# Half a block of split-precision weights beside each attention unit: the sparse queries' projection and half of the output projection moved

## The chip, the core and the metric

One core of a Trainium2 chip runs the whole program. The metric is the time of one execution in microseconds (us) on the device. Engines: TensorE (PE, its weight loads PEld), VectorE (DVE), ScalarE (ACT), GpSimd (POOL) and SyncE (SP), which issues nearly all transfers.

## The reference, cut to what matters

A decoder trunk of two layers over 272 tokens (16 meta tokens and 256) of width 2048, in float32:

```python
proj = h @ w_in        # u | fq fk fv | ff | dq | ckv | iq ik iw
y_ssm = _s5_mixer(u, ...)                    # state space, then a gate g @ glu_w
y_fox = _fox_attention(fq, fk, fv, ff)       # 8 heads of 64, forgetting bias
dk, dv = jnp.split(_rms_norm(ckv) @ w_kv_up, 2)
dq, dk, iq, ik = (_partial_rope(t) for t in (dq, dk, iq, ik))
y_dsa = _dsa_attention(dq, dk, dv, iq, ik, iw, topk=64)   # keys chosen by an indexer
y = concat(rms(y_ssm), rms(y_fox), rms(y_dsa))            # 1024 | 512 | 512
h = layer_norm(ALPHA * h + y @ w_out)
h = layer_norm(ALPHA * h + conv_ffn(h))      # up, causal conv, silu gate, down
```

The softmax of the forgetting attention subtracts a row's maximum, so a term that is the same for every key of a row drops out of it.

## The kernel before, in words

Activations lie with features on the partitions and the 272 tokens along the free axis. All weights come as one stream of blocks of 512 KB (`stream`, in the order of use): a block holds 4 tiles of 128 input features (KB) for 256 output features. Four slots (`raw`) take the blocks in turn. The table `PHASES` gives each phase's output groups and blocks for each group: `in` 17 x 4, `glu` 4 x 2, `out` 8 x 4, `up` 44 x 4, `down` 8 x 11.

For the phases in `SPLIT` the product is made in three parts: ACT rounds the block to `w_hi` (`cast`, L699), DVE makes the remainder (`low_part`, L992), and PE does for each of 4 tiles and 2 halves lo x hi, hi x lo and hi x hi (`split_block`, L383 to L385): 24 matmuls of 128 x 272 for a block. They add up in two PSUM banks. `glu` uses the raw block in plain float32 (L587).

The order of work on each engine is written out by hand, and semaphores tie the engines together. A layer runs:

1. **Input projection with the state space beside it.** 18 steps; the loop deals 4 blocks of `in` to each of the first 16 steps, and puts between them the state space products of chunk m (L424, L434, L456, L465, L470), the rope matmuls (`ROPE_STEPS`, L496, DVE L1290 to L1293) and the products with `w_kv` (L510). Ropes 9 to 12 are those of the sparse queries dq, 13 to 16 those of the sparse keys, in steps 16 and 17, after the last block.
2. **Indexer and gate.** 48 index scores (L575) and four gate groups (L587).
3. **Attention in 48 units**, 24 of the forgetting kind and then 24 of the sparse kind: 8 heads, each with three query tiles of 96, 96 and 80 rows against 96, 192 and 272 keys. PE does for unit n the scores (L522 to L527, or L530 and L531), the transposes of unit n-2's probabilities (L543) and unit n-3's weighted values (L554). DVE takes the maximum (L1455), scales it (L1457), copies the transposed probabilities from PSUM (L1466), and inverts the denominator (L1469). ACT does the exponential (L888) and stores the output (L897). Beside this DVE picks the top 64 keys for each query in eight rounds (`top_scores`, L1404 and L1407), one in every third unit of the first 24, makes `dsa_bias` from them (`sparse_bias`), and normalises the gated output `yssm` (L1487), ACT and DVE splitting it in two parts (`high_part`, `low_y`). Weights stand still in this stage.
4. **Output projection** (`products` with phase `out`): 8 groups of 4 blocks, the first two blocks of each on the gated half of y, the third on the forgetting, the fourth on the sparse outputs. DVE's `residual` (L1083, L1087, L1100) adds ALPHA times the old h, which is kept as x_hi and x_lo, and sums h over the first 12 tiles in `hsum`. PE sums that over the partitions (L369) after group 6; DVE subtracts this pivot (`take_pivot`, L1015) and folds squares (L1025 to L1029), before the residual of group 7.
5. The layer norm, the MLP (`up`, `down`), and the second layer norm.

The first forgetting score product of a unit is followed by `pe.matmul(s, cum[:, qs:ke], sel_r...)` (L524), which adds the query's own cumulative gate to each key, and by L525, which subtracts the key's.

## Time and profile before

| | us |
|---|---|
| median of 3 runs | 2813.67 (2808.85 to 2813.9) |
| the profiled execution's own time | 2811.41 |
| its span, first to last instruction | 2809.6 |
| PE busy | 2668.1 (95%) |
| PEld busy | 2548.4 (91%) |
| DVE busy | 1782.2 (63%) |
| ACT busy | 1366.1 (49%) |
| mean granted TensorE clock | 0.938 |

The durations of matmuls overlap, since they are pipelined: what one costs in a dense stretch is the distance from its start to the next one's. The granted clock is a share of 2.4 GHz: 1.00 is 2.4, 0.50 is 1.2 GHz. The two layers pass the same stages, the second some 1400 us after the first.

### The profile page before, as it was taken

What the parts mean: (1) busy time and instruction counts of PE and PEld (TensorE: products, weight loads), DVE (VectorE), ACT (ScalarE), POOL (GpSimd) and SP (SyncE); (2) the same over time, 40 slices, a digit from 0 to 9 for tenths busy, and PEclk for the clock granted to TensorE, in tenths of its full rate; (3) what the DMA queues carried; (4) which work ended last, traced back from release to release, by engine and by line L of the source; (5) the groups of instructions that cost most, each with busy time, mean ns of one, the idle gap of its engine ahead of it and who ended that gap; (6) DMA issues with size and microseconds to landing.
All of it is one profiled execution on the core that took longest, in us unless ns stands there. A gap on an engine that the chain in (4) does not pass through costs nothing.

```text
span 2809.6 us, 56056 instructions
## 1 busy us (share of the span) xinstructions
PE 2668.1 (95%) x21786; PEld 2548.4 (91%) x21786; DVE 1782.2 (63%) x2890; ACT 1366.1 (49%) x2051; POOL 11.9 (0%) x19
## 2 busy tenths in 40 slices
PE   5989999989999999999979899999899999999997
PEld 5989866989999999999979898669899999999997
DVE  6777555576666666544487775655766666665445
ACT  5444443456555555433364444444566665653333
POOL 0000000000000000000000000000000000000000
PEclk8999975899999999999999999659999999999999
DMA  4433210435555555554444332104355555555553
GB/s 170 146 113 127 76 45 1 150 120 179 179 173 177 172 173 171 180 173 166 165 146 150 107 127 77 38 1 163 115 194 182 182 180 179 184 184 186 173 183 112
DMA packets 109728, 401.84 MB, mean 143 GB/s; under 512 B 12176, under 2 KB 12176, under 8 KB 109584
## 3 DMA queue, kind: packets, MB, share of 16 engines
q1 hardware_dynamic: 108432, 395.15, 41.9%
q0 software_dynamic: 1152, 4.63, 0.4%
q8 instruction: 108, 1.77, 0.3%
q14 instruction: 36, 0.29, 0.0%
HBM read 397.50 MB, written 2.23 MB: 142 GB/s over the span
## 4 chain that ended last, share of the span: by engine, by line
PE 89%; DVE 6%; ACT 3%; issue 2%; DMA 1%; SPq 0%; ACTq 0%; DVEq 0%
PE ps L383 25%; PE ps L384 25%; PE ps L385 25%; PE ps L587 2%; PE ps L554 2%; PE ps L530 1%; PE ps L456 1%; PE ps L522 1%; PE ps L575 1%; PE ps L543 1%; PE ps L465 1%; DVE h L1047 1%; DVE h L1067 1%; ACT h L715 1%; PE ps L531 1%
## 5 line engine op out<-in xcount | busy, mean ns | idle before, releaser
L699 ACT ACTIVATE w_hi<-raw 128x1024 fp32r<-128x1024 f32 x728 | 763.6, 1057 | 935.3 <-PE ps L385 918.0
L384 PE MATMUL ps<-x_lo,w_hi 128*128 128x272 f32 (+1 forms) x3904 | 1122.1, 287 | 0.0
L385 PE MATMUL ps<-x_hi,w_hi 128*128 128x272 f32 (+1 forms) x3904 | 1120.2, 287 | 0.0
L992 DVE TENSOR_TENSOR w_lo<-raw,w_hi 128x1024 fp32r<-128x1024 f32 x592 | 716.8, 1224 | 616.3 <-ACT w_hi L699 616.2
L383 PE MATMUL ps<-x_hi,w_lo 128*128 128x272 f32 (+1 forms) x2816 | 805.5, 286 | 19.9 <-DVE x_lo L1075 19.3
L384 PEld LDWEIGHTS ps<-x_lo,w_hi 128*128 128x128 f32 x3904 | 741.3, 190 | 1.8
L385 PEld LDWEIGHTS ps<-x_hi,w_hi 128*128 128x128 f32 x3904 | 741.1, 190 | 0.0
L383 PEld LDWEIGHTS ps<-x_hi,w_lo 128*128 128x128 f32 x2816 | 530.8, 189 | 21.8 <-issue 19.2
L383 PE MATMUL ps<-g_hi,w_lo 128*128 128x272 f32 (+1 forms) x1408 | 403.9, 287 | 4.8 <-DVE w_lo L992 2.7
L384 PE MATMUL ps<-g_lo,w_hi 128*128 128x272 f32 (+1 forms) x1408 | 403.2, 286 | 0.0
L385 PE MATMUL ps<-g_hi,w_hi 128*128 128x272 f32 (+1 forms) x1408 | 401.2, 285 | 0.0
L383 PEld LDWEIGHTS ps<-g_hi,w_lo 128*128 128x128 f32 x1408 | 266.9, 190 | 5.3 <-DVE w_lo L992 2.9
L385 PEld LDWEIGHTS ps<-g_hi,w_hi 128*128 128x128 f32 x1408 | 268.3, 191 | 0.0
L384 PEld LDWEIGHTS ps<-g_lo,w_hi 128*128 128x128 f32 x1408 | 266.8, 189 | 0.2
L383 PE MATMUL ps<-x_hi,in_lo_a 128*128 128x272 f32 x544 | 169.2, 311 | 23.6 <-DVE x_lo L1075 15.3
L383 PE MATMUL ps<-x_hi,in_lo_b 128*128 128x272 f32 x544 | 163.6, 301 | 0.0
L1532 DVE SCALAR_TENSOR_TENSOR conv<-ps,cpar,conv 128x271 f32<-128x271 f32 (+1 forms) x352 | 159.4, 494 | 3.1
L383 PE MATMUL ps<-y_hi,w_lo 128*128 128x272 f32 x512 | 150.4, 294 | 0.7 <-DVE w_lo L992 0.7
L385 PE MATMUL ps<-y_hi,w_hi 128*128 128x272 f32 x512 | 149.5, 292 | 0.0
L383 PEld LDWEIGHTS ps<-x_hi,in_lo_a 128*128 128x128 f32 x544 | 107.8, 198 | 27.4 <-issue 25.0
L992 DVE TENSOR_TENSOR in_lo_b<-raw,w_hi 128x1024 fp32r<-128x1024 f32 x68 | 83.2, 1224 | 67.9 <-ACT w_hi L699 67.7
L383 PEld LDWEIGHTS ps<-x_hi,in_lo_b 128*128 128x128 f32 x544 | 102.2, 188 | 5.4 <-issue 3.2
(257 smaller groups left out, 2977.6 us busy)
## 6 DMA issues: line engine op xcount, KB each, us to landing
raw<-stream SPq DMA_DIRECT2D x744, 512.0 KB, 3.3
h<-x SPq DMA_DIRECT2D x4, 544.0 KB, 6.2
out<-h SPq DMA_DIRECT2D x4, 544.0 KB, 2.7
cst<-consts POOLq DMA_DIRECT2D x2, 724.0 KB, 6.4
wkv<-w_kv POOLq DMA_DIRECT2D x2, 512.0 KB, 7.8
b_st<-ssm_b POOLq DMA_DIRECT2D x2, 512.0 KB, 9.2
c_st<-ssm_c POOLq DMA_DIRECT2D x2, 512.0 KB, 11.4
par<-params SPq DMA_DIRECT2D x1, 562.0 KB, 12.0
```

Source lines behind the costliest of these rows:

```text
L383: pe.matmul(acc, lo_w[:, kk, cols], hi, start=k == 0, stop=False)
L384: pe.matmul(acc, w_hi[:, slot, kk, cols], lo, start=False, stop=False)
L385: mm = pe.matmul(acc, w_hi[:, slot, kk, cols], hi, start=False, stop=k == tiles - 1)
L456: mm = pe.matmul(ps[:, 4 + e, c * NJ:c * NJ + NJ], abt[rows, s, c, :], proj[rows, U0 + m, s * NJ:s * NJ + NJ], start=s == 0, stop=s == CH - 1)
L465: pe.matmul(ps[:, 6, k * NJ:NT], kexp[:, k, :, :].rearrange("p e q -> p (e q)"), proj[:, U0 + m, 0:(CH - k) * NJ], start=k == 0, stop=False)
L522: pe.matmul(s, proj[b, FQ0 + hd // 2, qs:ke], proj[b, FK0 + hd // 2, 0:ke], start=True, stop=False)
L530: pe.matmul(s, proj[b, DQ0 + hd // 2, qs:ke], kv[b, hd // 2, 0:ke], start=True, stop=False)
L554: mm = pe.matmul(ps[0:qn, 7, 0:HEAD], pt[0:kn, n % 2, q - c, 0:qn], v_tok[0:kn, kind, c, hd * HEAD:hd * HEAD + HEAD], start=c == 0, stop=c ...
L587: mm = pe.matmul(ps[:, 2 * (g % 2) + j, 0:NT], raw[:, n % SLOTS, kk, j * P:j * P + P], proj[:, U0 + k, :], start=k == 0, stop=k == 7)
L699: act.activation(w_hi[:, slot, :, :], raw[:, slot, :, :], ACT.Copy).then_inc(hi_made, 1)
L992: dve.tensor_tensor(w_low(phase, slot), raw[:, slot, :, :], w_hi[:, slot, :, :].bitcast(F32), ALU.subtract).then_inc(in_lo_made if phase = ...
L1532: last = dve.scalar_tensor_tensor(out=cv[:, j, tap:NT], in0=ps[:, 2 * odd + j, 0:NT - tap], scalar=cpar[:, odd, 2 + 2 * tap + j:3 + 2 * ta ...
```

## The change

Eight of the 68 blocks of the input projection, those of the sparse queries dq, become a phase `late` (2 groups of 4 blocks); the output projection is cut into a phase `gated` (8 groups of 2 blocks, the gated half of y) and `out` (8 groups of 2, the attended half). Both new phases run inside attention: beside each unit PE does half a block, `late` in units 0 to 15, `gated` in units 16 to 47. ACT casts and DVE makes low parts one or two units ahead, into three areas `gated_w` and not `w_lo`, and one pair of PSUM banks, 0 and 1, takes all these groups. ACT moves a finished `late` group to `proj` in units 7 and 15, and the four dq ropes follow in units 9, 10, 17 and 18. DVE ends each `gated` group with the ALPHA terms of the residual, so that `out` adds only its own sum. The input projection then runs in 17 steps that take 7 blocks in two. In the first 24 units the copy of the transposed probabilities goes from DVE to ACT, the maximum is negated in the same instruction (the scale 1/8 goes into the queries when PSUM is read, and the factor 8 in `sel` is dropped), and L524's product is removed. Line numbers of the changed kernel are higher: 407 to 409 answer to 383 to 385, 1063 to 992.

```diff
-PHASES = {"in": (17, DT // KB, 1), "glu": (4, UT // KB, 4), "out": (8, DT // KB, 4),
-          "up": (FT, DT // KB, 2), "down": (8, FT // KB, 4)}
-SPLIT = ("in", "out", "up", "down")
+PHASES = {"in": (15, DT // KB, 1), "glu": (4, UT // KB, 4), "late": (2, DT // KB, 2), "gated": (8, UT // KB, 4),
+          "out": (8, UT // KB, 4), "up": (FT, DT // KB, 2), "down": (8, FT // KB, 4)}
...
+
+
+def blocks_at(step, pos):
+
+    n = 4 + 7 * (step // 2) + 4 * (step % 2) + pos
+    return [n] if n < BLOCKS_IN and not (step % 2 and pos == 3) else []
+
...
+
+ROPE_STEPS = {6: (0,), 7: (1, 2), 8: (3, 4), 9: (5, 6), 10: (7, 8), 15: (9, 10), 16: (11, 12)}
 ROPES = 17
-MS_STEP = 5
-KV_STEPS = {12: (0, 1), 13: (2, 3), 14: (4, 5), 15: (6, 7)}
+LATE_ROPES = {9: 13, 10: 14, 17: 15, 18: 16}
+MS_STEP = 6
+KV_STEPS = {11: (0, 1), 12: (2, 3), 13: (4, 5), 14: (6, 7)}
...
+GATED_FROM = 16
 FOX_NORM = UNITS // 2 + 3
...
+            def late_half(l, n):
+
+                g, b = n // 8, n // 2 % 4
+                if n % 8 == 0:
+                    pe.wait_ge(psum_free, first_group(l, "late") + g + 2)
+                pe.wait_ge(lo_made, first_low(l, "late") + n // 2 + 1)
+                split_block("late", (first_block(l, "late") + n // 2) % SLOTS, b, 0, DT, x_parts, part=range(2 * (n % 2), 2 * (n % 2) + 2))
+
+            def gated_half(l, n):
+
+                g, b = n // 4, n // 2 % 2
+                if n % 4 == 0:
+                    pe.wait_ge(psum_free, first_group(l, "gated") + g + 2)
+                pe.wait_ge(lo_made, first_low(l, "gated") + n // 2 + 1)
+                split_block("gated", (first_block(l, "gated") + n // 2) % SLOTS, b, 0, UT, lambda k: (y_hi[:, k, :], y_lo[0][:, k, :]),
+                            (lambda k: (ylo_made, 4 * l + k // 4 + 1)) if n < 4 else None, part=range(2 * (n % 2), 2 * (n % 2) + 2))
+
+            def late_rope(l, r):
+
+                pe.wait_ge(roped, l * ROPES + r)
+                if r == 13:
+                    pe.wait_ge(glu_sd, l + 1)
+                pe.wait_ge(psum_free, first_group(l, "late") + (r - 13) // 2 + 1 + 2)
+                pe.matmul(ps[:, rope_bank(r), 0:NT], const("perm"), rope_tile(r), start=True, stop=True).then_inc(rot_made, 1)
...
-                    pe.matmul(s, cum[:, qs:ke], sel_r[:, hd:hd + 1].to_broadcast([P, ke]), start=False, stop=False)
...
+                    if n < GATED_FROM:
+                        late_half(l, n)
+                    elif n < UNITS:
+                        gated_half(l, n - GATED_FROM)
+                    if n in LATE_ROPES:
+                        late_rope(l, LATE_ROPES[n])
                     if 2 <= n < UNITS + 2:
...
+                    act.activation(dst, src, ACT.Copy, scale=SCALE if FQ0 <= 2 * g < FQ0 + 4 else 1.0).then_inc(psum_free, 1)
...
+                def half_cast(n):
+
+                    if n % 2 == 0:
+                        if n < GATED_FROM:
+                            cast(l, "late", n // 2)
+                        else:
+                            cast(l, "gated", (n - GATED_FROM) // 2)
...
+                    if 2 <= n < UNITS // 2 + 2:
+                        m = n - 2
+                        q = m % NQ
+                        qn = QT[q][1]
+                        act.wait_ge(ptr_made, l * UNITS + m + 1)
+                        if m >= 2:
+                            act.wait_ge(o_made, l * UNITS + m - 1)
+                        act.activation(pt[0:MASK_T, m % 2, 0:q + 1, 0:qn],
+                                       ps[0:MASK_T, 6, 0:NQ * MASK_T].rearrange("p (c t) -> p c t", c=NQ)[:, 0:q + 1, 0:qn],
+                                       ACT.Copy).then_inc(pt_made, 1)
...
+                        high_part((n - GATE_NORM - 6) // 2)
+                    if n in (7, 15):
+                        g = n // 8
+                        act.wait_ge(block_used, first_block(l, "late") + 4 * (g + 1))
+                        act.activation(proj[:, DQ0 + 2 * g:DQ0 + 2 * g + 2, :], ps[:, 0:2, 0:NT], ACT.Copy, scale=SCALE).then_inc(psum_free, 1)
+                    if n < UNITS - 4:
+                        half_cast(n + 4)
...
                 blocks = PHASES[phase][1]
+                bank = 0 if phase == "gated" else 2 * (g % 2)
                 dve.wait_ge(block_used, first_block(l, phase) + blocks * (g + 1))
-                h2 = h[:, 2 * g:2 * g + 2, :]
-                dve.scalar_tensor_tensor(out=h2, in0=x_lo[:, 2 * g:2 * g + 2, :].bitcast(F32), scalar=ALPHA,
-                                         in1=ps[:, 2 * (g % 2):2 * (g % 2) + 2, 0:NT],
-                                         op0=ALU.mult, op1=ALU.add).then_inc(psum_free, 1)
-                dve.wait_ge(psum_free, first_group(l, phase) + g + 3)
-                mark(dve.scalar_tensor_tensor(out=h2, in0=x_hi[:, 2 * g:2 * g + 2, :].bitcast(F32), scalar=ALPHA, in1=h2,
-                                              op0=ALU.mult, op1=ALU.add))
-                if g < PIVOT // 2:
+                h2, acc = h[:, 2 * g:2 * g + 2, :], ps[:, bank:bank + 2, 0:NT]
+                if phase == "out":
+                    dve.tensor_tensor(h2, h2, acc, ALU.add).then_inc(psum_free, 1)
+                    dve.wait_ge(psum_free, first_group(l, phase) + g + 3)
+                else:
+                    dve.scalar_tensor_tensor(out=h2, in0=x_lo[:, 2 * g:2 * g + 2, :].bitcast(F32), scalar=ALPHA,
+                                             in1=acc, op0=ALU.mult, op1=ALU.add).then_inc(psum_free, 1)
+                    dve.wait_ge(psum_free, first_group(l, phase) + g + 3)
+                    mark(dve.scalar_tensor_tensor(out=h2, in0=x_hi[:, 2 * g:2 * g + 2, :].bitcast(F32), scalar=ALPHA, in1=h2,
+                                                  op0=ALU.mult, op1=ALU.add))
+                if g < PIVOT // 2 and phase != "gated":
...
-                        after()
-                        dve.tensor_scalar(stat[0:qn, 0, n % 4:n % 4 + 1], stat[0:qn, 0, 4 + n % 4:5 + n % 4], -SCALE, None,
-                                          ALU.mult).then_inc(max_made, 1)
+                        dve.reduce_max(stat[0:qn, 0, n % 4:n % 4 + 1], ps[0:qn, S_BANKS[n % 3], 0:qs + qn], AX_X,
+                                       negate=True).then_inc(max_made, 1)
                     if n >= 2:
                         m = n - 2
...
-                        if m >= 2:
+                        if m >= UNITS // 2:
+                            dve.wait_ge(ptr_made, l * UNITS + m + 1)
                             dve.wait_ge(o_made, l * UNITS + m - 1)
-                        dve.tensor_copy(pt[0:MASK_T, m % 2, 0:q + 1, 0:qn],
-                                        ps[0:MASK_T, 6, 0:NQ * MASK_T].rearrange("p (c t) -> p c t", c=NQ)[:, 0:q + 1, 0:qn]
-                                        ).then_inc(pt_made, 1)
+                            dve.tensor_copy(pt[0:MASK_T, m % 2, 0:q + 1, 0:qn],
+                                            ps[0:MASK_T, 6, 0:NQ * MASK_T].rearrange("p (c t) -> p c t", c=NQ)[:, 0:q + 1, 0:qn]
+                                            ).then_inc(pt_made, 1)
+                        else:
+                            dve.wait_ge(prob_made, l * UNITS + m + 1)
...
-                    if GATE_NORM + 4 <= n < GATE_NORM + 12:
-                        k = n - GATE_NORM - 4
-                        last = dve.scalar_tensor_tensor(out=yssm[:, k, :], in0=yssm[:, k, :], scalar=param("mix_g", l * DT + k),
-                                                        in1=rstd[:, :], op0=ALU.mult, op1=ALU.mult)
+                    if GATE_NORM + 4 <= n < GATE_NORM + 8:
+                        for k in range(2 * (n - GATE_NORM - 4), 2 * (n - GATE_NORM - 4) + 2):
...
+                    if n < UNITS - 2:
+                        half_low(n + 2)
+                    if n in LATE_ROPES:
+                        dve.wait_ge(roped, l * ROPES + LATE_ROPES[n])
+                        rope(LATE_ROPES[n])
+                    if n >= GATED_FROM and n % 4 == 3 and n < UNITS:
+                        residual(l, "gated", (n - GATED_FROM) // 4)
...
-                for g in range(8):
-                    for n in range(4):
-                        if g:
-                            low_part(l, "out", 4 * g + n)
-                    if g:
+                for g in range(1, 9):
+                    for n in range(2):
+                        if g < 7:
+                            low_part(l, "out", 2 * g + 2 + n)
+                    if g < 8:
                         residual(l, "out", g - 1)
```

**PE, one unit of the forgetting kind** (the widest query tile): before, its scores, a transpose of unit n-2, and the values of unit n-3.

```order
L522 MATMUL ps<-proj 80x272
L524 MATMUL ps<-sel_r,cum 80x272
L525 MATMUL ps<-cum,sel_r 80x272
L527 MATMUL ps<-causal_r,ident_r 80x80
L543 MATMUL ps<-cst,probs 96x96
L554 MATMUL ps<-v_tok,pt 80x64 x3
```

Now, unit 9, a narrow one, of the changed kernel (L571, L573, L575 are its scores, L560 is a late rope, L591 and L602 transposes and values; the three dense rows come four times):

```order
L571 MATMUL ps<-proj 96x96
L573 MATMUL ps<-cum,sel_r 96x96
L575 MATMUL ps<-causal_r,ident_r 96x96
L407 MATMUL ps<-x_hi,gated_w_73 128x272
L408 MATMUL ps<-x_lo,w_hi 128x272
L409 MATMUL ps<-x_hi,w_hi 128x272
...
L560 MATMUL ps<-proj,cst 128x272
L591 MATMUL ps<-cst,probs 96x96 x2
L602 MATMUL ps<-v_tok,pt 96x64
```

Twelve dense matmuls stand between the scores and the transposes, and one small matmul is gone.

**DVE, unit 8**, before:

```order
L1455 TENSOR_REDUCE stat<-ps 80x1
L1457 TENSOR_SCALAR stat<-stat 80x1
L1466 COPY pt<-ps 96x96
L1469 RECIPROCAL stat<-stat 96x1
L1404 MAX top_88<-work 96x8 x2
L1404 MAX top_88<-work 80x8
L1407 MATCH_REPLACE work<-top_88,work 96x96
L1407 MATCH_REPLACE work<-top_88,work 96x192
L1407 MATCH_REPLACE work<-top_88,work 80x272
L1487 SCALAR_TENSOR_TENSOR yssm<-yssm,par,rstd 128x272
```

and now:

```order
L1538 TENSOR_REDUCE stat<-ps 80x1
L1552 RECIPROCAL stat<-stat 96x1
L1477 MAX top_92<-work 96x8 x2
L1477 MAX top_92<-work 80x8
L1480 MATCH_REPLACE work<-top_92,work 96x96
L1480 MATCH_REPLACE work<-top_92,work 96x192
L1480 MATCH_REPLACE work<-top_92,work 80x272
L1570 SCALAR_TENSOR_TENSOR yssm<-yssm,par,rstd 128x272 x2
L1063 TENSOR_TENSOR gated_w_74<-raw,w_hi 128x1024
```

The scaling and the copy have left; a second normalising product and a low part have come, all ahead of unit 9's maximum.

**DVE, the end of the output projection**, before:

```order
L1100 TENSOR_TENSOR hsum<-hsum,h 128x544
L992 TENSOR_TENSOR w_lo<-raw,w_hi 128x1024 x4
L1083 SCALAR_TENSOR_TENSOR h<-x_lo,ps 128x544
L1087 SCALAR_TENSOR_TENSOR h<-x_hi,h 128x544
L1015 SCALAR_TENSOR_TENSOR h<-ps,h 128x1088 x3
L1015 SCALAR_TENSOR_TENSOR h<-ps,h 128x544
L1025 TENSOR_TENSOR sq_out<-sq_out 128x1088 x2
```

and now:

```order
L1063 TENSOR_TENSOR w_lo<-raw,w_hi 128x1024 x2
L1156 TENSOR_TENSOR h<-h,ps 128x544
L1175 TENSOR_TENSOR hsum<-hsum,h 128x544
L1156 TENSOR_TENSOR h<-h,ps 128x544
L1086 SCALAR_TENSOR_TENSOR h<-ps,h 128x1088 x3
L1086 SCALAR_TENSOR_TENSOR h<-ps,h 128x544
L1096 TENSOR_TENSOR sq_out<-sq_out 128x1088 x2
```

The pivot and the squares are unchanged, and the residual ahead of them has one operation where it had two.

## Rows read from the trace of the kernel before

**Rows 1.** Windows by stage; columns: length, busy by engine, PEclk, DMA share, GB/s

```profile
core 0: us, PE busy (x) PEld busy (x) DVE busy (x) ACT busy (x) POOL busy (x), PEclk, DMA share, GB/s
60.00:323.30 263.30, 251.33 (x2768) 241.74 (x2768) 198.13 (x293) 113.79 (x180) 0.00 (x0) 0.99 0.37 126
323.30:380.90 57.60, 53.40 (x334) 40.76 (x332) 23.02 (x67) 26.35 (x70) 0.00 (x0) 1.00 0.19 65
380.90:498.80 117.90, 111.77 (x496) 80.65 (x496) 70.09 (x308) 49.73 (x167) 0.00 (x0) 0.51 0.02 5
504.70:600.00 95.30, 95.30 (x738) 94.98 (x739) 58.74 (x68) 34.28 (x33) 0.00 (x0) 0.97 0.52 177
```

**Rows 2.** Timeline of PE: three forgetting units late in the stage; start, length

```profile
425.26 0.95 PE L522 MATMUL ps<-proj 64*96 64x192 f32 x2
...
427.82 1.19 PE L522 MATMUL ps<-proj 64*80 64x272 f32 x2
...
429.55 0.38 PE L543 MATMUL ps<-cst,probs 96*96 96x96 f32 x1
...
432.44 0.95 PE L522 MATMUL ps<-proj 64*96 64x192 f32 x2
```

**Rows 3.** Timeline of PE: the first three units, before the clock falls

```profile
380.87 0.38 PE L522 MATMUL ps<-proj 64*96 64x96 f32 x2 [1.05 <-ACT yssm L838]
...
382.45 0.68 PE L522 MATMUL ps<-proj 64*80 64x272 f32 x2
383.06 0.34 PE L524 MATMUL ps<-sel_r,cum 128*80 128x272 f32 x1
383.24 0.29 PE L525 MATMUL ps<-cum,sel_r 128*80 128x272 f32 x1
383.38 0.20 PE L527 MATMUL ps<-causal_r,ident_r 80*80 80x80 f32 x1
```

**Rows 4.** Timeline of PE: from one sparse unit to the third after it

```profile
475.60 0.63 PE L530 MATMUL ps<-kv,proj 64*96 64x96 f32 x2
...
481.90 0.63 PE L530 MATMUL ps<-kv,proj 64*96 64x96 f32 x2
```

**Rows 5.** Timeline of PE: dense matmuls in the input projection, 21 starts apart

```profile
100.74 0.29 PE L385 MATMUL ps<-x_hi,w_hi 128*128 128x272 f32 x1
...
103.35 0.28 PE L385 MATMUL ps<-x_hi,w_hi 128*128 128x272 f32 x1
```

**Rows 6.** Timeline of PE: dense matmuls as the output projection begins, three starts apart

```profile
505.52 0.43 PE L383 MATMUL ps<-y_hi,w_lo 128*128 128x272 f32 x1
...
506.20 0.43 PE L383 MATMUL ps<-y_hi,w_lo 128*128 128x272 f32 x1
```

**Rows 7.** The page's groups, and DVE's timeline: casts, low parts, a round of the top keys

```profile
L699 ACT ACTIVATE w_hi<-raw 128x1024 fp32r<-128x1024 f32 x728 | 763.6, 1057 | 935.3 <-PE ps L385 918.0
L992 DVE TENSOR_TENSOR w_lo<-raw,w_hi 128x1024 fp32r<-128x1024 f32 x592 | 716.8, 1224 | 616.3 <-ACT w_hi L699 616.2
...
430.58 0.84 DVE L1404 MAX8 top<-work 96x8 f32<-96x96 f32 x3
...
432.30 1.28 DVE L1447 TENSOR_TENSOR gated_lo<-yssm,y_hi 128x1088 fp32r<-128x1088 f32 x1
```

**Rows 8.** Timeline of PE and of DVE: the end of the output projection

```profile
591.88 1.08 PE L369 MATMUL ps<-hsum,ones_p 128*128 128x272 f32 x4
...
595.95 4.32 DVE L1015 SCALAR_TENSOR_TENSOR h<-ps,h 128x1088 f32<-128x1088 f32 x4
...
603.73 0.72 DVE L1029 TENSOR_TENSOR sq_out<-sq_out 128x544 f32<-128x544 f32 x1
604.98 0.72 DVE L1083 SCALAR_TENSOR_TENSOR h<-x_lo,ps 128x544 f32<-128x544 f32 x1 [0.53 <-PE ps L385]
```

**Rows 9.** A window of 3 us inside the input projection

```profile
168.00:171.00 3.00, 1.91 (x15) 1.62 (x14) 2.93 (x5) 2.48 (x3) 0.00 (x0) 1.00 0.57 175
```

**Rows 10.** Timeline of PE: the wait for the sparse bias

```profile
441.42 0.64 PE L530 MATMUL ps<-kv,proj 64*96 64x96 f32 x2 [3.01 <-DVE dsa_bias L1420]
```

188 lines of the change are left out of this document (97 added, 91 removed).

## Prediction

> **What bounds the kernel now.** I read the stages first, then the starts on TensorE inside them. The windows by stage [rows 1] show PE busy for 251 of 263 us in the input projection, and for all of 95 us in the output projection, at a granted clock near 1.00: there the path is PE's stream of dense matmuls, and DVE (198 of 263) and ACT (114) have room. In attention PE is busy for 112 of 118 us too, but the clock is 0.51, and DVE (70) and ACT (50) are half idle, and almost nothing is loaded. So attention is bound by small matmuls at 1.2 GHz. Three units of the forgetting kind take 432.44 - 425.26 = 7.18 us [rows 2], three sparse ones 6.30 [rows 4].
>
> The clock was 1.00 through the indexer stage [rows 1]. The first units still ran at it: the widest tile's four score products take from 382.45 to 383.58, 1.13 us [rows 3]; the same products late in the stage take from 427.82 to 429.55, 1.73 us [rows 2]. So a unit at full clock takes 1.13 / 1.73 = 0.65 of its time at half clock.
>
> A dense matmul costs (103.35 - 100.74) / 21 = 0.124 us at full clock [rows 5], a block of 24 of them 2.98. At half clock it costs (506.20 - 505.52) / 3 = 0.227 [rows 6].
>
> **The change part by part**, for one layer, then doubled (the second layer runs the same code; only its MLP differs).
>
> *Input projection.* 8 blocks leave: 8 x 2.98 = -23.9. Four rope matmul pairs leave, about as long as the widest plain float32 score product (382.45 to 383.06, 0.6 [rows 3]): -2.4. PE was busy 95% of the stage, so most of this is on the path, but the state space work on DVE stays, with one low part less (1.22 [rows 7]) in each pair of steps, and PE has to wait for its results sooner. 3 us inside the stage show how that looks: PE busy 1.91, DVE 2.93 [rows 9]. I give back 2. Together -25; the bounds are -18 (each pair of steps keeps a further us) and -28 (all of it, and a shorter tail with two dk ropes behind the last block in place of four).
>
> *Output projection.* 16 blocks leave: 16 x 2.98 = -47.8. Two things come late now. After group 6, PE sums the pivot (591.88, 1.08), and DVE then subtracts it and folds squares from 595.95 to 604.45 (603.73 + 0.72), 8.5 us, before the residual of group 7; that residual waited only 0.53 more for PE, which had 12 us of group 7 to do [rows 8]. Group 7 is now 6 us. PE is ready at 591.9 + 1.1 + 6.0 = 599.0, DVE at 593.1 + 8.5 = 601.6: 2.6 us come back, less 0.7 for a residual that has one operation. At the beginning only one block, not three, covers the split of the sparse outputs: +1. Together -45, bounds -47 and -41.
>
> *Attention.* Each unit gets 12 dense matmuls: 12 x 0.124 = 1.49 us at full clock. If PE then does 1.49 of dense work in each unit I expect the clock to stay at 1.00, because in the input projection it did, where small products alternate with dense blocks and PE has gaps such as the one in [rows 9]. The rest of a unit shrinks: forgetting, without L524 (0.18 [rows 3]): 7.18 / 3 x 0.65 - 0.18 = 1.38; sparse: 6.30 / 3 x 0.65 = 1.37. The values and transposes behind the scores have no row at full clock; if they did not shrink at all, a unit would be about 0.35 longer, if all halved with the clock 0.35 shorter. Unit: 2.87 against 2.39 and 2.10. So 24 x (0.48 + 0.77) = +30.
>
> Around the units: at the start PE's first dense half waits for two casts and a low part, 2 x 1.06 + 1.22 = 3.3 [rows 7], which had no place on the path before. Four late ropes: +2.4. DVE gets 24 low parts (29.4), 16 residual operations of 0.72 (11.5, by the nearest such row [rows 8]) and four ropes, and loses 48 scalings and 24 copies; in total some 101 of 156 us, which is room, but it comes in bursts. In unit 8 stand a round of the top keys (430.58 to 432.30, 1.7 [rows 7]), two normalising products, a low part and the maximum, some 4.7 us against a unit of 2.9; units 6 to 11 add up to about 20 us on DVE against 17 on PE. PE meets it when it needs the next exponential: +5 for all such stalls, those for the single pair of dense PSUM banks included. The wait for the sparse bias, 3.0 [rows 10], gets shorter since PE has 1.5 us of dense work ahead of it: -1.5. The pieces at start and end run faster: -1. ACT gets 24 casts (25.4) and 24 copies, some 85 of 155 us: hidden, since it only has to stay a unit ahead. Transfers: 24 blocks of 512 KB in 155 us is 81 GB/s, where the output projection took 177 [rows 1]; the stage moved almost nothing before. Sum: 30 + 3.3 + 2.4 + 5 - 1.5 - 1 = +38, stage 156 us for 118. Bounds: +20 and +65.
>
> **Sum**: -25 - 45 + 38 = -32 for a layer, -64 for both. The profiled execution took 2811.4 (span 2809.6, 1.8 around it; 2.3 below the median of the runs shown): 2811.4 - 64 = 2747, and I say 2748.
>
> **A rule against the trace.** The window row has PE busy for 95% of attention and yet 0.51 of the clock [rows 1]: busy time by the records is not what holds the clock. The Trainium skill (TensorE: Matmul & The Clock Gate, "Part 1: The HAM clock gate") says that the clock gate follows how busy PE has been, and its "Part 4: PE-mode transpose" that transposes do not count as busy in the same way. By the first alone, attention should have run at 2.4 GHz already, and the change could gain only the idle 6 us in it: against this the row decides. The second would leave a unit's transposes out on both sides of the change, and speaks for the first rival.
>
> **Rivals.**
>
> 1. *The clock stays at 1.2 GHz in attention: slower.* Dense matmuls then take 12 x 0.227 = 2.72 a unit and the rest is not shortened: 2.39 - 0.3 + 2.72 = 4.8 and 2.10 + 2.72 = 4.8. 48 x 4.8 = 231 where 108 stood, +123, with 8 around it +131; -25 - 45 + 131 = +61 for a layer, 2811 + 122 = 2933. For it: with a mean of 0.51 over 118 us [rows 1] the clock fell in the first few, in units much like those that remain. Against it: half of each unit's PE time is now dense work, over which the long stages show 0.97 and 0.99 [rows 1]. It decides when more than about a third of the stage is at half clock (a layer's 32 us over the 93 that the half clock costs).
> 2. *DVE or its bursts set the unit.* Units of 3.4 us, not 2.87, and 25 us more in a layer: 2798. For it: the order around units 6 to 11, where each maximum queues behind the extra work, and ACT's copy of unit n-2 behind the exponential of unit n. Against it: DVE has a third of the stage free in total.
> 3. *The input projection gives nothing*, since DVE's state space chain, not PE, sets a pair of steps: -8 in place of -25, 2747 + 34 = 2781. Against it: 95% PE [rows 1].
> 4. *PE's small work shrinks fully with the clock*, and the bursts hide: unit 2.5, 17 us less in a layer: 2714.
>
> **How the numbers follow.** The forecast with its own spread, 0.58; rival 1, 0.10; rival 2, 0.12; rival 3, 0.08; rival 4, 0.12. The range has to leave out rival 1 and the far ends of rivals 2 and 4: 2708 to 2802. A measurement of this kernel can tell some 0.2% (5.6 us) from no change. Slower: rival 1 and the end of rival 2, 0.12. Same: where rivals 2 and 3 meet, 0.04. Faster: 0.84.
>
> **What would show it.** Right: the attention window some 156 us long with PEclk at 0.95 or more; dense starts 0.124 us apart in it; the input projection about 25 us shorter and the output projection about 45; a wait of some 2 us at its end for DVE's fold. Wrong: PEclk 0.50 in attention with dense starts 0.227 apart (rival 1); DVE busy over 90% with PE waiting for the exponential or the copy in most units (rival 2); windows of the input projection with PE busy under 85% (rival 3).

## The result and the profile after

| | before | changed |
|---|---|---|
| median, us | 2813.78 (2808.85 to 2813.9, 4 runs) | 2782.14 (2780.16 to 2782.92, 4 runs) |
| ratio, 95% interval | | 0.9891 [0.9874, 0.9908] |
| span of the profiled execution | 2809.6 | 2778.3 |
| mean granted TensorE clock | 0.938 | 0.966 |

The kernel is faster by 31.6 us, or 1.1%. The forecast was 66 less than before: the sign and the range held, the size is a little under half of what was said. The page after, its first lines:

```profile
span 2778.3 us, 55896 instructions
## 1 busy us (share of the span) xinstructions
PE 2608.2 (94%) x21738; PEld 2503.6 (90%) x21738; DVE 1762.5 (63%) x2762; ACT 1376.7 (50%) x2097; POOL 11.9 (0%) x19
```

I cut both layers at the same events: the last dense block of the input projection, the first attention score, the last weighted value, the first product of the output projection, the first product of the norm's sums (so PE's wait ahead of it counts to the output projection), the first dense product of the MLP. The first layer, us:

| stage | before | changed | difference | forecast |
|---|---|---|---|---|
| input projection, ends at | 323.3 | 302.9 | -20.4 | -25 |
| from there to the first score | 57.5 | 63.5 | +6.0 | 0 |
| attention | 117.9 | 161.9 | +44.0 | +38 |
| last transposes | 5.9 | 5.9 | 0 | 0 |
| output projection | 101.1 | 56.6 | -44.5 | -45 |
| norm behind it | 13.6 | 14.2 | +0.6 | in the -45 |

Together -14.3; the second layer gives -15.7 in the same places (its attention +41.7). The windows of these stages in the changed kernel, which answer to [rows 1], and then five stretches inside them. Columns as there: length, busy of PE, PEld, DVE, ACT, POOL, granted clock, DMA share, GB/s.

```profile
60.00:302.90 242.90, 225.36 (x2553) 215.05 (x2552) 185.30 (x276) 102.47 (x168) 0.00 (x0) 0.98 0.36 119
302.90:366.40 63.50, 58.02 (x331) 43.06 (x329) 21.96 (x64) 26.28 (x70) 0.00 (x0) 0.92 0.18 59
366.40:528.30 161.90, 150.68 (x1056) 130.24 (x1056) 99.46 (x288) 82.58 (x217) 0.00 (x0) 0.92 0.25 82
534.20:590.80 56.60, 51.50 (x393) 50.79 (x393) 39.40 (x51) 22.34 (x22) 0.00 (x0) 0.98 0.45 149
170.00:180.00 10.00, 6.24 (x30) 6.04 (x31) 9.52 (x22) 4.13 (x8) 0.00 (x0) 0.66 0.17 61
314.00:326.00 12.00, 11.08 (x34) 7.69 (x34) 4.03 (x12) 5.54 (x16) 0.00 (x0) 0.57 0.01 1
366.40:374.00 7.60, 4.58 (x22) 3.92 (x22) 3.66 (x7) 5.65 (x8) 0.00 (x0) 0.78 0.55 171
443.00:459.00 16.00, 15.91 (x85) 13.48 (x83) 5.81 (x15) 6.11 (x17) 0.00 (x0) 0.68 0.18 57
484.00:500.00 16.00, 12.91 (x58) 10.79 (x59) 5.88 (x18) 3.29 (x9) 0.00 (x0) 0.57 0.11 34
```

The clock in attention rose from 0.51 [rows 1] to 0.92, so the main premise held. But it is not 1.00, and what is missing is not spread out: it lies in a few stretches, with full clock between them. Ahead of each such stretch stands a pause of PE. The timeline of PE in the changed kernel, the rows with an idle time in brackets ahead of them:

```profile
173.76 1.25 PE L521 MATMUL ps<-proj,cst 128*128 128x272 f32 x2 [4.62 <-DVE proj L1368]
...
305.05 0.70 PE L521 MATMUL ps<-kv,cst 128*128 128x272 f32 x2 [1.52 <-DVE kv L1368]
...
312.71 1.41 PE L623 MATMUL ps<-proj 64*96 64x96 f32 x6 [0.77 <-ACT v_tok L876]
315.04 4.78 PE L623 MATMUL ps<-proj 64*96 64x96 f32 x18 [0.92 <-ACT v_tok L876]
...
370.10 0.56 PE L407 MATMUL ps<-x_hi,gated_w 128*128 128x272 f32 x1 [2.98 <-DVE gated_w L1063]
...
442.74 0.41 PE L578 MATMUL ps<-kv,proj 64*96 64x96 f32 x2 [1.50 <-DVE dsa_bias L1493]
...
486.15 0.87 PE L647 MATMUL ps<-cst,y_tok 96*128 96x96 f32 x4 [2.49 <-DVE proj L1512]
...
493.03 0.77 PE L647 MATMUL ps<-cst,y_tok 80*128 80x80 f32 x4 [0.94 <-DVE proj L1512]
```

They are, in order: a rope product in the input projection that waits for the rope before it; the last such rope; two transposes that wait for the values' copy behind the gelu; the first dense half block, which waits for its low part; the sparse bias; and the transposes of the forgetting outputs, which in the changed kernel all go to bank 2, so that each waits until DVE has read the last. Behind the pause of 2.49 the dense starts are 0.227 us apart (two of the three products of each chunk are shown):

```profile
488.62 0.43 PE L409 MATMUL ps<-y_hi,w_hi 128*128 128x272 f32 x1
488.84 0.43 PE L407 MATMUL ps<-y_hi,gated_w 128*128 128x272 f32 x1
...
489.30 0.43 PE L409 MATMUL ps<-y_hi,w_hi 128*128 128x272 f32 x1
```

Where no pause is near and nothing else stands between them, three forgetting units and three sparse ones take 411.57 - 403.13 = 8.44 and 469.56 - 461.40 = 8.16 us, 2.81 and 2.72 each (with the ropes, the gate's sum and the small waits, all units of a kernel below that keeps full clock, b3_all, average 2.95 and 2.84):

```profile
403.13 0.68 PE L571 MATMUL ps<-proj 64*80 64x272 f32 x2
...
411.57 0.68 PE L571 MATMUL ps<-proj 64*80 64x272 f32 x2
...
461.40 0.68 PE L578 MATMUL ps<-kv,proj 64*80 64x272 f32 x2
...
469.56 0.68 PE L578 MATMUL ps<-kv,proj 64*80 64x272 f32 x2
```

**Theories.** A: a pause of PE costs its own length and then more, since PE runs at 1.2 GHz for a while behind it. B: a pause costs its own length; the stretches at half clock have another cause, or fall by chance, and units are dearer than forecast.

### The profile page after: what moved, and what is told of

Its sections match the earlier page's. It is cut to its first block, busy times and chain, and to the rows that moved or that the text cites. A ratio compares the mean times of both kernels' runs of the same rounds, so it can differ in the third digit from the quotient of the medians.

```text
span 2778.3 us, 55896 instructions
## 1 busy us (share of the span) xinstructions
PE 2608.2 (94%) x21738; PEld 2503.6 (90%) x21738; DVE 1762.5 (63%) x2762; ACT 1376.7 (50%) x2097; POOL 11.9 (0%) x19
## 4 chain that ended last, share of the span: by engine, by line
PE 87%; DVE 7%; ACT 3%; issue 2%; DMA 1%; SPq 0%; ACTq 0%; DVEq 0%
PE ps L407 25%; PE ps L408 25%; PE ps L409 25%; PE ps L635 2%; PE ps L481 1%; PE ps L623 1%; PE ps L602 1%; PE ps L578 1%; PE ps L490 1%; PE ps L571 1%; DVE h L1138 1%; DVE h L1118 1%; ACT h L761 1%; PE ps L495 1%; DMA raw<-stream 1%
## 5 line engine op out<-in xcount | busy, mean ns | idle before, releaser
L745 ACT ACTIVATE w_hi<-raw 128x1024 fp32r<-128x1024 f32 x728 | 762.4, 1056 | 818.0 <-PE ps L409 795.9
L1063 DVE TENSOR_TENSOR w_lo<-raw,w_hi 128x1024 fp32r<-128x1024 f32 x560 | 677.6, 1224 | 571.8 <-ACT w_hi L745 571.6
L407 PE MATMUL ps<-x_hi,w_lo 128*128 128x272 f32 (+1 forms) x2816 | 805.8, 286 | 18.7 <-DVE x_lo L1146 18.4
L407 PE MATMUL ps<-x_hi,in_lo_a 128*128 128x272 f32 x480 | 149.2, 311 | 21.8 <-DVE x_lo L1146 15.5
L1622 DVE SCALAR_TENSOR_TENSOR conv<-ps,cpar,conv 128x271 f32<-128x271 f32 (+1 forms) x352 | 159.4, 494 | 3.1
L407 PE MATMUL ps<-x_hi,in_lo_b 128*128 128x272 f32 x480 | 144.6, 301 | 0.6 <-DVE in_lo_b L1063 0.6
L407 PEld LDWEIGHTS ps<-x_hi,in_lo_a 128*128 128x128 f32 x480 | 94.0, 196 | 27.7 <-issue 22.3
L409 PEld LDWEIGHTS ps<-y_hi,w_hi 128*128 128x128 f32 x512 | 102.5, 200 | 0.0
L407 PEld LDWEIGHTS ps<-x_hi,in_lo_b 128*128 128x128 f32 x480 | 91.6, 191 | 4.2 <-issue 1.6
L1014 ACT ACTIVATE gate<-conv 128x272 f32<-128x272 f32 x88 | 38.0, 432 | 114.8 <-DVE conv L1622 114.8
## 6 DMA issues: line engine op xcount, KB each, us to landing
c_st<-ssm_c POOLq DMA_DIRECT2D x2, 512.0 KB, 11.2
```

The source lines that it names most:

```text
L407: pe.matmul(acc, lo_w[:, kk, cols], hi, start=k == 0, stop=False)
L409: mm = pe.matmul(acc, w_hi[:, slot, kk, cols], hi, start=False, stop=k == tiles - 1)
L745: act.activation(w_hi[:, slot, :, :], raw[:, slot, :, :], ACT.Copy).then_inc(hi_made, 1)
L1014: act.activation(gate[:, odd, :], conv[:, odd, 1, :], ACT.Silu).then_inc(gate_made, 1)
L1063: dve.tensor_tensor(w_low(phase, slot), raw[:, slot, :, :], w_hi[:, slot, :, :].bitcast(F32), ALU.subtract).then_inc(in_lo_made if phase = ...
L1622: last = dve.scalar_tensor_tensor(out=cv[:, j, tap:NT], in0=ps[:, 2 * odd + j, 0:NT - tap], scalar=cpar[:, odd, 2 + 2 * tap + j:3 + 2 * ta ...
```

## Experiments: one pause at a time

Four kernels, each with one edit to the changed kernel.

*The rope alone (a1_rope)*: in odd steps the second rope product stands ahead of the step's last block.

```diff
-                        in_blocks(l, blocks_at(step, 2))
                         side_products(l, step, 1)
+                        in_blocks(l, blocks_at(step, 2))
```

> The changed kernel, and in the odd steps of the input projection the second rope or w_kv product now stands ahead of the step's last block instead of behind it, so that a block (3.0 us) lies again between one rope and the next. Theory A (pauses: each wait of PE of some us costs its own length, and then several us at half clock): the two waits of 4.6 and 4.2 us for DVE's rope in a layer shrink below 2 us together, the stretches at half clock behind them go, and the input projection's window gets 8 to 13 us shorter in each layer: 2756 to 2766 us for 2782. Theory B (DVE's state space chain sets the pair of steps, and the wait only moves): window within 2 us, time 2778 to 2783.

*The gelu alone (a2_gelu)*: seven of the eight tiles pass the gelu before the last chunk's outputs are read.

```diff
+                    if step == STEPS - 1:
+                        act.wait_ge(y_read, UT * (l + 1) - 1)
+                        act.activation(proj[:, 0:UT - 1, :], proj[:, 0:UT - 1, :], ACT.Gelu_apprx_tanh)
...
-                act.activation(proj[:, 0:UT, :], proj[:, 0:UT, :], ACT.Gelu_apprx_tanh).then_inc(gelu_made, 1)
+                act.activation(proj[:, UT - 1:UT, :], proj[:, UT - 1:UT, :], ACT.Gelu_apprx_tanh).then_inc(gelu_made, 1)
```

> The changed kernel, with the gelu of the first seven of the eight tiles taken by ACT before the last chunk's outputs instead of behind them. Theory A: V's copies no longer wait for 3.3 us of table load and gelu, PE no longer pauses 0.8 and 0.9 us among the first index scores, the half clock behind them goes, and the stage from the last dense block to the first attention score falls from 63.5 to 57 to 60 us: 4 to 6 us in each layer, 2770 to 2775 us. Theory B (the clock there falls because of the ropes and transposes, not of the pause): 1.5 us in each layer, 2779.

*The first dense blocks alone (a3_first)*: their casts and the first low part are made before the last gate group ends.

```diff
+                    if g == 3:
+                        cast(l, "late", 0)
+                        cast(l, "late", 1)
                     gate_out(g)
...
-                for n in range(4):
-                    half_cast(n)
...
+                    if n == 47:
+                        low_part(l, "late", 0)
...
-                for n in range(2):
-                    half_low(n)
```

> The changed kernel, with the casts and the low part of the first dense blocks made before the last gate group has ended. Theory A: PE's 3.0 us wait at the first dense half goes, and the 3 us at half clock behind it: attention's window falls from 161.9 by 4 to 5 us, 2772 to 2775 us. Theory B (whatever comes next is late too: the first exponentials, and the sum of the gate squares): below 2 us in each layer, 2779 to 2782.

*The reads alone (a4_reads)*: DVE reads a forgetting output from bank 2 at the head of the unit, not at its end.

```diff
                 for n in range(UNITS + 2):
+                    if FOX_NORM + 9 <= n < FOX_NORM + 12:
+                        output_read(0, n - FOX_NORM - 9)
...
-                    if FOX_NORM + 9 <= n < FOX_NORM + 12:
-                        output_read(0, n - FOX_NORM - 9)
```

> The changed kernel, with DVE's reads of the forgetting outputs' transposes, which now share one PSUM bank, at the head of the next unit instead of at its end. Theory A: PE's waits of 2.5 and 0.9 us for the bank go, and with them 14 us at half clock (486 to 500 in the profile): three units of 4.5 us become units of 2.8, so attention's window is 7 to 10 us shorter, 2762 to 2769 us. Theory B (a wait costs its length only): 3.4 us in each layer, 2775.

| | median (runs), us | ratio to before, 95% | attention, layers 1, 2 | up to the first score, layers 1, 2 |
|---|---|---|---|---|
| changed | 2782.1 (2780.2 to 2782.9) | 0.9891 [0.9874, 0.9908] | 161.9, 159.6 | 63.5, 63.4 |
| a1_rope | 2767.9 (2763.1 to 2772.5) | 0.9843 [0.9827, 0.9859] | 157.6, 155.4 | 58.4, 56.8 |
| a2_gelu | 2764.8 (2763.2 to 2771.8) | 0.9835 [0.9818, 0.9852] | 159.2, 155.1 | 56.6, 56.6 |
| a3_first | 2765.9 (2763.5 to 2768.7) | 0.9832 [0.9816, 0.9849] | 148.8, 152.9 | 63.3, 63.5 |
| a4_reads | 2765.9 (2764.1 to 2770.2) | 0.9828 [0.9812, 0.9845] | 151.9, 153.0 | 63.3, 63.4 |

Each takes away 1.5 to 3.4 us of PE's waits in a layer, and each gains 14 to 17 us in two. For the rope it is not the place that I had named: the input projection still ends at 302.8 in the first layer, the waits there only stand elsewhere. The gain came behind it: 5.1 and 6.6 us up to the first score, where the last rope's wait of 1.5 us went, and 4.3 and 4.2 us in attention, whose waits it leaves as they were. And that four edits so unlike gave nearly one figure could have been chance, a stretch at half clock that falls or doesn't. The table also shows edits acting where they were not made: a2_gelu too leaves every wait of the attention stage as it was, and that stage is still 2.7 and 4.5 us shorter. a2_gelu and a3_first came out below the 2770 to 2775 and 2772 to 2775 of theory A. So the next four ran with the changed kernel once more among them (b0_after). Two are again single edits: DVE's top-k rounds and the bias two units earlier (b1_top), and PE's pivot sum one block earlier with three of DVE's four steps of it ahead of the residual of group 6 (b2_pivot). The last (b3_all) has all six.

```diff
-                    if n % 3 == 2 and n // 3 < TOPK // 8:
+                    if n % 3 == 0 and n // 3 < TOPK // 8:
...
-                    if n == 3 * (TOPK // 8) - 1:
+                    if n == 3 * (TOPK // 8) - 3:
```

```diff
+                            if phase == "out" and g == 2 and b == 0:
+                                pe.wait_ge(h_summed, it * body + (PIVOT // 2 * 2 * l + 2))
+                                for k in range(2):
+                                    mm = pe.matmul(ps[:, 4, 0:NT], ones[:, :], hsum[:, k, :], start=k == 0, stop=k == 1)
+                                mm.then_inc(pivot_made, 1)
...
+                    if g == 7:
+                        for c in range(3):
+                            take_pivot(ln, c)
                     if g < 8:
                         residual(l, "out", g - 1)
-                for c in range(4):
-                    take_pivot(ln, c)
+                take_pivot(ln, 3)
```

> The changed kernel again, unchanged, beside the others: the four variants before this one differ in what they edit and all came to 2765 to 2768 us. Theory A (each pause of TensorE of some us costs its own length and several us at 1.2 GHz behind it, in places that are fixed for a given program): 2782 again, span 2778, the same two stretches at half clock in the attention stages (8 to 12 us each at about 443 to 459 and 484 to 500). Theory B (the stretches at half clock fall by chance, run by run): a time between 2765 and 2790 and other stretches at half clock; then most of the 14 to 17 us of each variant would be chance.

> The rounds of VectorE's top-k (max, match-replace) come two units earlier, so the bias wait of 1.50 us at 442.7 in each layer goes. Theory A: the wait and the some 5 us lost at half clock behind it go too, 6 us per layer, 12 in all: 2768 to 2774. Theory B (a pause costs only its own length): 3 us in all: 2778 to 2780.

> TensorE's sum for the pivot stands one block earlier and three of VectorE's four steps of it stand ahead of the last residual, so that TensorE's wait of 3.25 us at the end of the output projection falls to about 1 us. Theory A: 2.3 us of wait and 1 to 3 us of the norm's eight matmuls at half clock per layer: 2771 to 2776. Theory B: the chain on VectorE only moves; the wait stays at 3 us and nothing is gained, 2780 to 2783.

> All six edits together (late rope pair ahead of the last block, seven tiles of the gelu early, casts of the first dense blocks early, early reads of the forgetting outputs, early top-k rounds, early pivot). Theory A: the pauses that start stretches at half clock are nearly gone in the attention stage; input projection -3, indexer stage -5, attention -8, norm -3 per layer, 19 per layer and 38 in all: 2740 to 2750, granted clock in the attention stage at least 0.97. Theory B: the edits share one gain of about 15 us that any change of the timing brings: 2760 to 2768.

| | median (runs), us | ratio to before, 95% | attention | norm |
|---|---|---|---|---|
| b0_after | 2780.7 (2778.9 to 2781.7) | 0.9893 [0.9872, 0.9914] | 161.8, 158.2 | 14.2 |
| b1_top | 2774.8 (2771.9 to 2778.9) | 0.9870 [0.9848, 0.9893] | 155.9, 158.3 | 14.5, 14.2 |
| b2_pivot | 2779.1 (2777.1 to 2785.1) | 0.9895 [0.9871, 0.9919] | 161.8, 159.4 | 13.0 |
| b3_all | 2727.6 (2725.4 to 2728.3) | 0.9704 [0.9684, 0.9724] | 143.1, 143.0 | 13.0 |

b0_after stands where the changed kernel stood, and in the first layer its stretches at half clock lie at the same places to within a few tenths of a us. In the second they do not. Input projection and attention of the second layer, of the changed kernel and then of b0_after, which is the same program:

```profile
1422.80:1689.20 266.40, 245.38 (x2687) 234.47 (x2688) 205.91 (x323) 121.14 (x197) 0.00 (x0) 0.97 0.35 116
1752.40:1912.00 159.60, 148.22 (x1056) 128.96 (x1056) 99.46 (x288) 82.52 (x217) 0.00 (x0) 0.94 0.25 83
```

```profile
1423.20:1692.40 269.20, 249.13 (x2687) 238.33 (x2688) 205.97 (x323) 121.10 (x197) 0.00 (x0) 0.95 0.34 114
1755.60:1913.80 158.20, 146.71 (x1056) 127.48 (x1056) 99.39 (x288) 82.44 (x217) 0.00 (x0) 0.95 0.25 84
```

So one stage of one program differs by 1.4 to 2.8 us from one execution to another, with the same matmuls. That is chance, but far less than the 14 to 17 us of each edit, and the two medians are 1.4 us apart: theory B falls in the form in which the gains are chance between executions. b1_top is in the middle, 6 us, and gains in one layer's attention only. b2_pivot shortens PE's wait ahead of the norm from 3.25 to 1.05 us, as forecast, but the pivot's products now stand in the output projection, which takes 56.5 us as before; only the norm falls, from 14.2 to 13.0, 2.4 us in two layers. Its median moved by 1.6, which is inside the spread and short of the 2771 to 2776 of theory A. b3_all gains 53 us on b0_after, much more than I expected, and its windows say why:

```profile
60.00:304.20 244.20, 226.96 (x2555) 217.39 (x2553) 186.41 (x279) 102.74 (x168) 0.00 (x0) 0.97 0.35 119
304.20:359.50 55.30, 52.29 (x329) 40.12 (x328) 21.78 (x62) 28.28 (x73) 0.00 (x0) 1.00 0.20 68
359.50:502.60 143.10, 139.21 (x1056) 121.01 (x1056) 97.86 (x287) 79.37 (x215) 0.00 (x0) 1.00 0.28 93
```

The granted clock is 1.00 through both stages. Of the 18.8 us that attention lost, 150.68 - 139.21 = 11.5 are PE busy for longer with the same 1056 matmuls (the clock), and the other 7.3 are idle time. Of the 8.2 between the input projection and the first score, 58.02 - 52.29 = 5.7 are the clock.

## Experiments: the price of one pause

In b3_all a pause can be put back alone. c2_notop, c3_noreads, d2_nofirst and d3_nogelu are b3_all, each with one of the six edits taken back: the top-k rounds, the reads, the first blocks, the gelu. d4_pause is c2_notop with more DVE work ahead of the bias:

```diff
                     if n == 3 * (TOPK // 8) - 1:
+                        for k in range(8):
+                            mark(dve.tensor_scalar(side[:, 1, :], side[:, 0, :], 0.0, None, ALU.mult))
+                            after()
                         sparse_bias()
```

> The version with six edits less the early top-k rounds: a single pause of 1.5 us of TensorE comes back at unit 24 of an attention stage that otherwise keeps full clock from its first unit to unit 68. The price of this one pause, per layer: theory A 1.5 plus 3 to 8 at half clock (stage 148 to 152 for 143.0; total 2737 to 2745); theory B 1.5 alone (stage 144.5; total 2731).

> The version with six edits less the early reads of the forgetting outputs: two pauses come back, 2.5 and 0.9 us at units 56 to 59. Theory A: 3.4 plus 5 to 9 at half clock per layer (stage 151 to 155 for 143.0; total 2744 to 2752); theory B: 3.4 alone (stage 146.5; total 2734).

> The version with six edits less the early casts and low part of the first dense blocks: TensorE again waits 3.0 us at its first dense matmul, at the head of the attention stage. Theory A: 3.0 plus 2 to 4 at half clock per layer (stage 148 to 150 for 143.0; total 2737 to 2742 for 2727.6). Theory B: 3.0 alone (stage 146; total 2734).

> The version without the early top-k rounds (2735.0 us, one pause of 1.5 us in the attention stage, cost 4.0 and 2.9 us in the two layers), with 8 more VectorE operations on 128x272 (some 3.5 us) right ahead of the bias, so that the pause is some 5 us. If what is lost behind a pause is fixed: 3.5 per layer more, stage 150 to 151, total 2742. If it grows with the pause in proportion: the pause of 5 costs 12, stage 155, total 2752.

> The version with six edits less the early gelu: two waits of 0.8 to 0.9 us for v_tok and whatever follows them come back between input projection and attention. If these 6 us of that stage are the gelu's: 61 to 63.5 for 55.3, total 2738 to 2744. If they were the late rope waits' (the variant with the rope alone also shortened this stage): 56 to 58, total 2729 to 2733.

| | median, us | ratio to before, 95% | PE's waits put back | attention | attention's cost over b3_all |
|---|---|---|---|---|---|
| b3_all | 2727.6 | 0.9704 [0.9684, 0.9724] | | 143.1, 143.0 | |
| c2_notop | 2735.0 | 0.9720 [0.9704, 0.9737] | 1.5 | 147.0, 145.9 | 3.9, 2.9 |
| c3_noreads | 2739.9 | 0.9738 [0.9722, 0.9754] | 2.5 and 0.9 | 147.6, 147.6 | 4.5, 4.6 |
| d2_nofirst | 2740.5 | 0.9753 [0.9734, 0.9772] | 3.0 | 149.9, 149.8 | 6.8, 6.8 |
| d4_pause | 2740.5 | 0.9752 [0.9735, 0.9770] | 4.2 | 150.4, 150.3 | 7.3, 7.3 |

The wait for the bias in c2_notop and in d4_pause, from the table of waits of PE in the attention stage (total, times, longest):

```profile
PE ps L583 <- DVE dsa_bias L1504: 1.5, 1, 1.5
```

```profile
PE ps L583 <- DVE dsa_bias L1504: 4.2, 1, 4.2
```

And the windows round the wait, of c2_notop and then of d4_pause:

```profile
426.00:450.00 24.00, 22.25 (x149) 19.50 (x147) 12.99 (x42) 10.88 (x32) 0.00 (x0) 0.86 0.22 68
```

```profile
426.00:450.00 24.00, 19.57 (x120) 17.40 (x120) 13.12 (x44) 8.84 (x25) 0.00 (x0) 0.79 0.20 66
```

Each of these pauses costs more than it is long, and the part on top is no multiple of it: 1.4 to 2.4 us for a pause of 1.5, 3.1 for one of 4.2, 3.8 for one of 3.0 at the head of the stage, 1.1 for two that sum to 3.4. So here a pause cost its length and 1 to 4 us. The proportional case of d4_pause (stage 155) is out, the fixed one (150 to 151) came. c3_noreads, at 147.6, is nearer to theory B (146.5) than to A (151 to 155).

Two cautions. The price is read from the stage, once in each layer, and not from the medians: the intervals of c2_notop and b3_all overlap, and the profile of c3_noreads is of its fastest execution (2734.0). And the stage varies by itself: it took 143.0 or 143.1 us in both layers of b3_all and of c1_rope2 (below), but 144.5 in the second layer of d3_nogelu and 146.1 in the first of d1_rope3, neither of which is edited there. The parts on top of d2_nofirst and d4_pause, 3.8 and 3.1, are as large as that or larger and the same in both layers; those of c2_notop and c3_noreads are not clear of it.

The three single prices add up to 15.2 and 14.3 us. The changed kernel lost 18.8 and 16.6, and b0_after 18.7 and 15.2: together they cost 1 to 4 us more than apart, which is hardly more than the stage's own variation.

Between the input projection and the first score the sum fails by more. PE's waits there are 1.5 for the last rope and 1.7 for the values behind the gelu; the edits a1, a2 and d3 leave them in singly:

| waits left in | kernel | stage, us |
|---|---|---|
| neither | b3_all | 55.3, 55.3 |
| rope 1.5 | a2_gelu | 56.6, 56.6 |
| values 1.7 | a1_rope, d3_nogelu | 58.4, 56.8 (both kernels) |
| both | changed | 63.5, 63.4 |

The rope's wait costs 1.3 alone, the values' 1.5 to 3.1, both together 8.2. d3_nogelu came to 2731.8 (0.9719 [0.9702, 0.9737]): the 6 us that I had not foreseen belong neither to the gelu nor to the rope but to the two within 10 us of each other. This sum is firmer than attention's: with both waits in, the stage took 63.1 to 63.5 us in each layer of all six kernels that have them (changed, b0_after, a3_first, a4_reads, b1_top, b2_pivot).

## Experiments: what waits in the input projection

In b3_all PE still waits 5.1 and 4.6 us for ropes in the input projection. DVE's timeline there shows it idle 2.16 us for ScalarE's cast, in a low part that stands ahead of the rope that PE wants:

```profile
169.38 0.72 DVE L1285 TENSOR_TENSOR rot<-rot,table 128x544 f32<-128x544 f32 x1
172.26 1.23 DVE L1072 TENSOR_TENSOR in_lo_b<-raw,w_hi 128x1024 fp32r<-128x1024 f32 x1 [2.16 <-ACT w_hi L750]
173.40 0.72 DVE L1293 TENSOR_TENSOR states<-rot 128x544 f32<-128x544 f32 x1
174.04 0.35 DVE L1258 SCALAR_TENSOR_TENSOR kexp<-cst,par,kexp 128x128 f32<-128x128 f32 x1
174.30 0.44 DVE L1374 TENSOR_TENSOR side<-ps,cst 128x272 f32<-128x272 f32 x1
```

c1_rope2 is b3_all with that rope ahead of the low part, in odd steps (the call in its old place is dropped there; the cut shows the new one):

```diff
                             turn_back()
+                        side_rope(step, 1)
                         lows(step, 2)
```

d1_rope3 moves the second rope of the even steps as well, ahead of `output_terms`.

```diff
                         lows(step, 1)
+                        side_rope(step, 1)
                         if live:
                             output_terms(l, m)
```

> All six edits, and besides VectorE applies the second rope of an odd step ahead of the low part that stands before it, where it idles 2.2 us for ScalarE's cast; TensorE's rope product then should no longer wait for it (waits of 5.1 us at 175.7 and 4.6 us at 214.0 in the version with six edits, 2727.6 us). Theory A: both waits fall to under 1 us and most of the input projection's 13.6 us at half clock goes: 8 of wait and 3 to 6 of clock per layer, 11 to 14 per layer, 2700 to 2706; input projection's end at 291 to 294 instead of 304.2. Theory B (a pause costs its own length alone, half-clock stretches stay): 8 per layer, 2712. If the wait only moves to the next rope: 2724 to 2728.

> The 2710.3 us version, with VectorE's second rope of an even step moved too, ahead of the output terms and the low part, so that the wait of 4.12 us at 192.3 in each layer should fall to under 1 us. Theory A (pause plus half clock behind it, 1.5 to 3 us here): 5 to 7 per layer, 2696 to 2701, input projection's end at 291 to 293. Theory B (length alone): 3.5 per layer, 2703. If the wait only moves to the state-space products that the rope now delays by 1.2 us: 2708 to 2711.

c1_rope2: 2710.3 us (2709.8 to 2712.4), 0.9633 [0.9617, 0.9649]; the input projection ends at 297.7 (295.7 after the layer's start in the second layer). The rope at 175.7 now stands at 171.6 and waits 0.81. But the next one grew: where b3_all waits 1.09 us for a rope, at 195.48, c1_rope2 waits 4.12, at 192.26. So part of the wait moved on, and 17 of the two layers' 22 to 28 us came; the time lies nearer to theory B's 2712 than to A's 2700 to 2706.

```profile
171.61 0.70 PE L526 MATMUL ps<-proj,cst 128*128 128x272 f32 x2 [0.81 <-DVE proj L1377]
...
192.26 1.25 PE L526 MATMUL ps<-proj,cst 128*128 128x272 f32 x2 [4.12 <-DVE proj L1377]
```

d1_rope3: 2715.1 (2714.3 to 2715.3), 0.9661 [0.9643, 0.9678]. The third case that I had written down came, the wait moves to the state space products, but the time is worse than the 2708 to 2711 that I gave for it.

```profile
194.81 3.35 PE L486 MATMUL ps<-proj,abt 32*128 32x68 f32 x64 [4.81 <-DVE proj L1377]
```

The chunk sums wait for the step's first rope, and DVE reaches that one only behind the scan of the forget gates and a low part. The first layer's input projection ends 1.9 us before c1_rope2's all the same, the second's takes 3.1 us longer, and its first attention stage took 146.1 us in place of 143.1. The same pause of 1.23 us stands 24 us into that stage in b3_all and in d1_rope3. Two windows of each, the pause and the 10 us behind it, b3_all and then d1_rope3:

```profile
379.40:384.40 5.00, 3.77 (x30) 3.14 (x29) 4.96 (x11) 3.86 (x13) 0.00 (x0) 1.00 0.25 96
384.40:394.40 10.00, 10.00 (x78) 8.76 (x77) 8.68 (x27) 5.49 (x13) 0.00 (x0) 1.00 0.21 66
```

```profile
371.00:376.00 5.00, 3.77 (x30) 3.14 (x29) 4.96 (x11) 3.87 (x13) 0.00 (x0) 1.00 0.28 86
376.00:386.00 10.00, 10.00 (x56) 9.06 (x55) 6.43 (x22) 3.92 (x10) 0.00 (x0) 0.66 0.18 65
```

PE was busy for 3.77 of 5 us in both, with the same 30 matmuls; behind it one ran at full clock and got through 78 matmuls in 10 us, the other at 0.66 and through 56. So a pause of some 1 us may pass free or cost 3, and which one it was changed between kernels that are alike in this stage and differ only ahead of it. The Trainium skill (TensorE: Matmul & The Clock Gate, "Part 1: The HAM clock gate") says that the window in which activity is looked at runs free of the kernel, so that the moment of a change varies with where work falls in it. That these two rows differ for this reason fits, but nothing here shows it.

## Experiment: what holds the clock

b4_sparse is the changed kernel with 2 of the 12 dense matmuls of each half block beside an attention unit left in (it leaves out most of the late projection and of the gated half of the output projection).

```diff
+                if phase in ("late", "gated"):
+                    for j in range(2):
+                        mm = pe.matmul(ps[:, bank + j, t0:NT], w_hi[:, slot, part[-1], j * P:j * P + P], rhs(b * KB + part[-1])[0][:, t0:NT],
+                                       start=True, stop=True)
+                    if KB - 1 in part:
+                        mm.then_inc(block_used, 1)
+                    return
```

> The changed kernel with 2 of the 12 matmuls of each half block beside an attention unit left in: it leaves out most of the late projection of the sparse queries and of the gated half of the output projection, every wait, cast, low part and read staying. If the dense work is what holds TensorE at full clock there, the granted clock of the attention stage falls to 0.50 to 0.6 as before the change, a unit takes 2.1 to 2.4 us though it has 1.2 us less to do, and the stage is 118 to 130 us. If the clock stays up for another reason, units take 1.6 to 1.7 us and the stage is 95 to 105 us.

```profile
366.50:512.10 145.60, 134.14 (x576) 101.00 (x576) 100.33 (x288) 81.42 (x217) 0.00 (x0) 0.53 0.28 91
```

One execution: 2750.6 us. With 576 matmuls in place of 1056 the stage takes 145.6 us in both layers, longer than b3_all's 143.1 with all of them, at a clock of 0.53. My number for the stage, 118 to 130, was too low: two dense matmuls at 0.227 us in 48 units are 22 us by themselves, and the waits at the start and for the reads stay. The mechanism is the one named: it is the dense work beside the small products that holds the clock. Against the changed kernel, which has nearly the same waits (the bias's is 1.5 there and 2.1 here), the 480 matmuls left out saved 161.9 - 145.6 = 16.3 us, 0.034 each, where one takes 0.124 in a dense stretch.

## Why the prediction was half right

**Right.** *The premise*: dense work beside each unit brings the stage to or near full clock (0.51 to 0.92, and 1.00 in b3_all). Rival 1, that it stays at 1.2 GHz, has its counterpart in b4_sparse. *The unit*: 2.87 forecast, 2.81 and 2.72 measured; the forecast is 0.06 to 0.15 too dear, some 5 us in 48 units. *The output projection*: -45 forecast, -44.5 and 0.6 in the norm. The wait at its end is there as said, for the residual behind DVE's fold, 3.25 us for 0.81 before, so 2.4 more where 2.6 less 0.7 were forecast (DVE's residual, then PE's sums of the norm behind it):

```profile
590.01 0.71 DVE L1156 TENSOR_TENSOR h<-h,ps 128x544 f32<-128x544 f32 x1
```

```profile
590.78 3.22 PE L433 MATMUL ps<-h,ones_p 128*128 128x272 f32 x8 [3.25 <-DVE h L1156]
```

*The single waits in attention*: 3.3 at the start was 3.0, the bias left at 1.5 was 1.50. DVE's 101 us of the stage were 99.5, and rival 2 did not come: PE's waits there are few and known by name, 11.2 us in 48 units.

**Wrong, by 16 to 18 us a layer.** Three steps of the sum:

1. *"I expect the clock to stay at 1.00"* and *"+5 for all such stalls"*. As lengths the stalls were right: PE idled 161.9 - 150.7 = 11.2 us in the stage, and 3.3 + 5 + 1.5 are 9.8. What the sum had no term for is the clock behind each: 11.5 us in this stage. I had priced every pause at its length. The reason given, that the clock stayed at 1.00 in the input projection though PE has gaps there, rested on a gap that had passed free ([rows 9]) and on a mean of 0.99 [rows 1]. The same trace holds one that did not: a wait of 3.41 us, with half clock round and behind it, in the very stage that was called as proof.

```profile
150.16 1.25 PE L496 MATMUL ps<-proj,cst 128*128 128x272 f32 x2 [3.41 <-issue]
```

```profile
148.70:155.60 6.90, 5.44 (x22) 5.24 (x23) 4.92 (x11) 1.35 (x2) 0.00 (x0) 0.51 0.23 76
```

   Of the stalls, the 3.4 us of the transposes that now share bank 2 were not named; the full diff showed them (`Y_BANKS` 1, 2, 1 to 2, 2, 2). That the stage's +38 came within 6 us of the +44.0 and +41.7 is in part luck: the clock that had no term stands against units that were too dear.
2. *"I give back 2"* in the input projection. It was 5.9 (-23.9 and -2.4 against the -20.4 measured), and most of it is length: PE's idle time in the stage rose from 12.0 to 17.5 us. No block stands any more between the second rope of an odd step and the first of the next, and DVE keeps a low part ahead of the rope that PE then waits for. c1_rope2 bears this out: with PE's product moved as in a1_rope and DVE's rope as well, the stage's end comes 25.6 and 27.6 us before that of the kernel before, the forecast's -25. a1_rope alone, which moved the product and not DVE's work, left the stage's end in the first layer where it was.
3. *No term between input projection and attention*, +6. The stage held the rope's wait of 1.52 us before the change too, and one of 0.59, at a clock of 1.00 [rows 1]:

```profile
328.39 1.16 PE L496 MATMUL ps<-kv,cst 128*128 128x272 f32 x4 [1.52 <-DVE kv L1293]
331.82 1.51 PE L566 MATMUL ps<-cst,kv 128*96 128x128 f32 x12 [0.59 <-DVE kv L1293]
```

   But then one rope stood ahead of the last chunk's outputs, which the gelu waits for, and the wait came behind them; now two ropes stand ahead of them, with the wait between. So the gelu starts 5.9 us behind the last dense block (308.77), where it started 3.6 behind it (326.95), while PE gets to the transposes after the same 6 us. What came are the waits of 0.77 and 0.92 for the values' copy behind the gelu. With the rope's they cost 5.7 us of clock: PE busy 58.02 us, where b3_all has 52.29.

Roughly, per layer: 11.5 and 5.7 of clock and 4.6 in the input projection, less the some 5 by which units were too dear, make 17.

**The rival that came nearest** was none of the four: rival 3 gives 2781, the time measured, for a reason that did not hold (the input projection gave 20.4, not 8).

## What to carry to other kernels

When a change brings TensorE to full clock, price every wait that is left or made in that stage at its length and, by the prices here, up to some 4 us more, and look for two that stand near each other first; take them away before judging the change. Here six small moves (casts, reads, a gelu, a rope, top-k rounds, the pivot) were worth 53 us, more than the change itself (no run has them without the change, so what they would give the kernel before is open), and c1_rope2, at 2710.3 us against 2782 and 2814, is the kernel to keep. Look at the windows inside a stage before calling its clock 1.00: a mean of 0.99 over 263 us hid 6.9 us at 0.51. And what leaves a stage leaves its cover too: list each operation that stood beside or ahead of the removed blocks, with who waits for it.

## What the runs showed that I had not expected

- Waits of PE of 1.5 and 1.7 us cost 1.3 and 1.5 to 3.1 us apart, and 8.2 together.
- The same wait of 1.23 us, with the same activity around it, was followed by a clock of 1.00 in one kernel and 0.66 in another. The changed kernel, profiled on two occasions, had its stretches at half clock in the same places in the first layer (attention 161.9 and 161.8 us) and in others in the second (159.6 and 158.2, input projection 266.4 and 269.2).
- Ten more dense matmuls in each of 48 units cost 16 us with all pauses in place: 145.6 us with 2 in a unit, 161.9 with 12. With 12 and nearly no pause the stage takes 143.1, less than with 2 and the pauses; 2 without pauses was not run.
